# A two-layer streaming encoder step: an opening that requests less, the indexer's and the selection's work laid out anew, and head loads of 128 partitions

## The chip, the cores and the metric

The program runs on one core of one Trainium2 chip. The metric is the device time of one execution in microseconds (us), the median of several. A profile of a single execution stands beside it. In what follows PE is TensorE, DVE is VectorE, ACT is ScalarE, POOL is GpSimd and SP is SyncE, which here issues nearly all DMAs. The profile counts 16 DMA engines for the core.

## The reference

One inference step of a trunk of two layers on two groups of rows: one prompt of 1024 rows, and 8 samples of 16 new rows (128 rows in all), each with 512 cached rows. The width is 1024.

```python
for layer in range(2):
    mod = silu(c) @ ada_w[layer] + ada_b[layer]
    shift, scale, gate = split(mod, 3)
    h = rms_norm(x, norm_g[layer]) * (1 + scale) + shift
    y = mixer(h)                 # layer 0: mixer_ab, layer 1: mixer_c
    x = x + gate * y
return rms_norm(x, final_norm_g)

def mixer_ab(h):                 # layer 0
    qa, ka, va, fa, ga, qb, kb, vb, iq, ik, iw, gb = split(h @ w_in)
    # A: 8 heads of 64, softmax(q k / 8 + cum_f[q] - cum_f[k]), causal
    # B: 8 heads of 64; indexer: score[q, k] = sum_h iw[q, h] * relu(iq[q, h] . ik[k]);
    #    the 256 best keys of a prompt row (132 of a sample row) are attended to
    return concat(oa * silu(ga), ob * silu(gb)) @ w_out
```

Layer 1 is a latent attention of 16 heads, which the change leaves alone. Keys, values, gates of forgetting and indexer keys are outputs too.

## The kernel before

All rows stand in 9 tiles of 128 (8 of the prompt, 1 of the samples). Products that need full precision are made of three passes, from a tensor split into a high and a low part (`product`, L274 to L276).
- **`opening`** loads the rows x, the first ada_w matrix (8 pieces of 1 MB, L114) and the weights of the first projection (`entry.fetch_weights`, L397). PE multiplies the pieces (L212), DVE places the modulation (L231, L234). Behind the weights SP also issues the rope tables (L116, L117), three more ada_w tiles through `Modulation.load` (L256 to L259, each after `w_used`), two short tables and a bias (L121 to L123).
- **`projection("ix")`** with `front=entry` makes the indexer's queries and keys. ACT first rounds weight pieces (`split_high`, L618), DVE subtracts (`split_low`, L694), four of eight pieces before the first row tile's `front.act` / `front.dve` and four behind it. PE turns row tiles (L317) and starts its products when all pieces are split. DVE applies rope (L843 to L846). Two MB of the modulation are multiplied beside it (L267).
- **`index_scores`** has 48 steps (6 row tiles, 8 heads): PE a product (L1020), ACT a relu (L1064), DVE a weighted sum (L1133). Between them stands the samples' work for batches b = 0 to 7, at steps given by dictionaries: PE turns cached keys at step 6+5b (L981), ACT and DVE split them at 7+5b (L1078, L1143), PE scores at 9+5b, ACT's relu at 10+5b, PE's sum at 11+5b (L995). The new keys' scores (24 products of 16 columns), their relu and sum stand behind the last step. ACT waits for the samples' queries and keys at step 5 (L1068).
- **`projection("ab")`** has 8 groups of 9 steps, in this order: copy, copy, copy, silu, rope, rope, copy, silu. A step is 24 products of PE; ACT moves a copy (L642) or makes the three passes of a silu (L648, L650, L652), DVE multiplies it (L718) or applies rope. Groups with a turned output (1, 2, 5 and 6) add four transposes, an ACT and a DVE operation (L674, L753) to each step. Beside this DVE runs the top-k selection, 7 row tiles wide: `idle` takes 4 of its 259 passes per step. 231 of them are counts of about 0.9 us (L1191) and the last 28, four per tile, turn the threshold into a mask (L1225 to L1238).
- **`branches_ab`** is the attention of layer 0: 16 heads g (8 of A, 8 of B), each with 8 row tiles of the prompt and one sample batch. SP loads, per head, queries and keys (`at_q`, `at_k`, L1338 and L1340; each half of the partitions holds the same 64 key rows, the halves of the queries are the high and low part), the decay row for A (L1344), values (L1347), cached keys (L1355), the additive row (`at_addt`, L1362), cached values (L1365) and the new values (L1366). Three buffers of queries and keys, two of the rest.
- Then come `mixed_out`, the projection, attention and output of layer 1.

The additive row is read through a pattern of the source whose outermost count is 8:

```python
rows = dram(c.s["negcum_s"], h * H * KEYS, [[KEYS, H], [0, TS], [1, KEYS]])   # H = 8, TS = 16
sp.dma_start(addt[:, g % 2], rows)
```

Of the kernel before, what the change touches and what calls it, by code (L numbers as in the profile page):

```python
# [7 lines left out]

# [13 lines left out]
P = 128  # L22
# [3 lines left out]
NB = 8  # L26
# [57 lines left out]
def opening(nc, c, x_tile, entry):  # L84

    S = lambda name: semaphore(nc, name)
    rows_in, g_in, bias_in, w_in, rope_in = S("mod_rows_in"), S("mod_g_in"), S("mod_bias_in"), [S(f"ada_w_in{i}") for i in range(AW)], S("rope_in")
# [6 lines left out]
    with ExitStack() as stack:  # L94
# [8 lines left out]
        def _(sp):  # L103
# [12 lines left out]
            sp.dma_start(c.ropeC[:], c.i["rope_cos"].rearrange("(i p) d -> p i d", p=P)).then_inc(rope_in, 16)  # L116
            sp.dma_start(c.ropeS[:], c.i["rope_sin"].rearrange("(i p) d -> p i d", p=P)).then_inc(rope_in, 16)  # L117
# [3 lines left out]
            sp.dma_start(c.ropeCs[:], c.i["rope_cos_short"].rearrange("(i p) d -> p i d", p=P)).then_inc(entry.tables_in, 16)  # L121
            sp.dma_start(c.ropeSs[:], c.i["rope_sin_short"].rearrange("(i p) d -> p i d", p=P)).then_inc(entry.tables_in, 16)
            sp.dma_start(c.fbias[:], dram(c.i["ab_f_bias"], 0, [[0, P], [1, H]])).then_inc(entry.tables_in, 16)  # L123
            sp.wait_ge(rope_in, 32)
# [27 lines left out]
        def _(act):  # L152
# [3 lines left out]
            for n in range(3):  # L156
# [7 lines left out]
                nc.scalar.activation(rstd[:, cols], ss[:, cols], ACT.Sqrt, scale=1.0 / D, bias=c.eps[:]).then_inc(std, 1)  # L164

# [56 lines left out]
AW = 3  # L222

# [146 lines left out]
class Entry(Rows):  # L370

    READY, SPLIT = 0, False

    def __init__(self, nc, c, w_dram, col, stack):
# [3 lines left out]
        self.w_hi, self.w_lo, self.tables_in = semaphore(nc, "ix_w_hi"), semaphore(nc, "ix_w_lo"), semaphore(nc, "tables_in")  # L378
# [5 lines left out]
    def place(self, side):  # L384
        sb = lambda n, shape, dt=F32: self.stack.enter_context(self.nc.sbuf_tensor(n, shape, dt))
        self.side = side
        with self.nc.sbuf_tensor("mod_x_first", [P, 2, D], F32) as self.x_first:
            pass
        self.T = sb("ix_T", [P, 2, 2, 4, P], F32R)
        self.x_rows = sb("mod_x_rows", [P, NT - 3, D])  # L390

# [7 lines left out]
    def enter(self, stack):  # L399
        super().enter(stack)  # L400
        self.wh = stack.enter_context(self.nc.sbuf_tensor("ix_wh0", [P, KT, 512], F32R))
# [17 lines left out]
class Front(Rows):  # L419

    READY, SPLIT = 1, True
# [50 lines left out]
def projection(nc, c, name, groups, idle=None, pair=BF16, ring=4, side=None, front=None, weights=None, sums=None):  # L472
# [36 lines left out]
    with ExitStack() as stack:  # L509
# [105 lines left out]
        def _(act):  # L615
# [3 lines left out]
            ahead = 0 if front and front.SPLIT else groups[0].kt  # L619
            for k in range(ahead // 2 if front else ahead):  # L620
                split_high(0, k)
            for i in range(2 if front else 0):
                front.act(act, i)
                if i == 0:
                    for k in range(ahead // 2, ahead):
# [57 lines left out]
        def _(dve):  # L683
# [11 lines left out]
            ahead = 0 if front and front.SPLIT else groups[0].kt  # L695
            for k in range(ahead // 2 if front else ahead):
# [3 lines left out]
            for i in range(2 if front else 0):  # L700
                front.dve(dve, i)
                if i == 0:
                    for k in range(ahead // 2, ahead):
                        split_low(0, k)
            for s in range(len(steps) + LAG):
                if front and s < len(steps):
                    front.dve(dve, s + 2)
                if s < len(steps) and groups[steps[s][0]].kind != "copy":
# [10 lines left out]
                    if kind == "rope":  # L719
                        rope(nc, chain, o, ps, turn[:, 0:n], c.ropeC[:, i, :], c.ropeS[:, i, :], n // DH, DH // 2).then_inc(nat_done, 1)  # L720
# [160 lines left out]
def index_scores(nc, c, sums, weights):  # L881
# [14 lines left out]
    turn_at, score_at, sum_at = {6 + 5 * b: b for b in range(NB)}, {9 + 5 * b: b for b in range(NB)}, {11 + 5 * b: b for b in range(NB)}  # L896
    high_at, relu_at = {7 + 5 * b: b for b in range(NB)}, {10 + 5 * b: b for b in range(NB)}
    NEW_ROW = 12
    assert max(sum_at) < N + 1
    with ExitStack() as stack:  # L900
# [57 lines left out]
        def _(pe):  # L958
# [45 lines left out]
            for s in range(N + 1):  # L1004
                if s < N:
                    i, h = steps[s]
                    m = s // H
                    if s == 0:
                        pe.wait_ge(k_done, 1)
# [1541 lines left out]
```

## Time and profile before

| | |
|---|---|
| median of 3 runs | 1937.97 us (1937.79 to 1943.93) |
| the profiled execution | 1940.82 us |
| its span, first to last instruction | 1939.1 us |
| mean granted TensorE clock | 0.940 |
| PE busy | 1689.8 us, 87% of the span |
| DVE busy | 1297.3 us, 67% |
| ACT busy | 941.7 us, 49% |
| DMA queue of SP and ACT, share of 16 engines | 38.3% |

The stages in the profile, by the times at which their first instructions start: opening 0 to 55.4 us, projection ix to 183, index_scores to 279.1, projection ab to 724.4, attention of layer 0 to 1049.4, the rest to 1939.1. A row of the list of DMA issues ends with the KB of one and, where the profile has it, the median time to landing. In a row of the timeline an engine name with a q (SPq) is its queue of issues; the text in brackets is the idle time before the instruction and what ended it. Granted clock 1.00 is 2.4 GHz, 0.50 is 1.2 GHz. A row of a window's sums holds its bounds, its length, the busy time (and count) of PE, PE's weight loads, DVE, ACT and POOL, and then the granted clock, the DMA share (mean busy share of the 16 DMA engines) and the GB/s that they moved.

### The profile page before, as it was taken

Reading aid. Unit: us, or ns where it says so; the run is one execution under the profiler, and the core shown is the slowest. Engines: PE = TensorE matmul, PEld = TensorE weight load, DVE = VectorE, ACT = ScalarE, POOL = GpSimd, SP = SyncE. Lnnn points to the kernel's source line nnn. Section 1 sums busy time; section 2 is a strip of 40 time slices with the busy share of each in tenths; the row PEclk is TensorE's granted clock in tenths of the full one; section 3 lists DMA queues with packets and bytes.
Section 4 is the critical chain, followed back from the end, with each engine's and each line's share of the span. In section 5 each row is a group of like instructions: output and inputs, shape, how many; then the busy total and the mean of one; then the engine's idle time right before and its main releaser. Section 6 shows DMA issues by size and latency. Waiting matters only on the chain. (4 is left out here: it accounts for less than half of the span.)

```text
span 1939.1 us, 34317 instructions
## 1 busy us (share of the span) xinstructions
PE 1689.8 (87%) x12754; PEld 1314.9 (68%) x12754; DVE 1297.3 (67%) x2825; ACT 941.7 (49%) x1897; POOL 209.0 (11%) x310
## 2 busy tenths in 40 slices
PE   3794789999998966899998998889996999999798
PEld 0572458888877854677776787677774776676687
DVE  0553577878999934678888655553365777777764
ACT  2422552227211364577876225447644676777421
POOL 2001100010000002101010000000004222221000
PEclk7797899999999987899998998989997999999899
DMA  9366511432233119968774643232235111111432
GB/s 347 116 211 191 121 39 51 130 105 88 74 98 107 62 55 223 227 195 217 198 197 147 230 172 119 70 110 96 73 79 117 28 28 45 27 28 51 152 130 98
DMA packets 229550, 235.17 MB, mean 121 GB/s; under 512 B 139350, under 2 KB 164214, under 8 KB 227339
## 3 DMA queue, kind: packets, MB, share of 16 engines
q1 hardware_dynamic: 222506, 213.07, 38.3%
q0 software_dynamic: 6880, 19.92, 2.8%
q8 instruction: 103, 1.69, 0.4%
q14 instruction: 61, 0.49, 0.1%
HBM read 173.98 MB, written 58.95 MB: 120 GB/s over the span
## 5 line engine op out<-in xcount | busy, mean ns | idle before, releaser
L274 PE MATMUL PS<-ab_wh,hT 128*128 128x512 f32 x576 | 231.4, 402 | 5.7 <-DVE ab_wl L694 5.7
L275 PE MATMUL PS<-ab_wl,hT 128*128 128x512 f32 x576 | 227.3, 395 | 0.0
L276 PE MATMUL PS<-ab_wh,hT 128*128 128x512 f32 x576 | 226.6, 393 | 0.0
L1191 DVE TENSOR_SCALAR_CACHE_REDUCE topk_junk<-scores,topk_small 128x528 bf16<-128x528 f32 (+6 forms) x224 | 194.6, 916 | 1.3
L2368 DVE CUSTOM_DVE_ANT_0 la_S<-PS,la_mask 128x128 f32<-128x128 f32 (+3 forms) x144 | 107.5, 747 | 41.5 <-PE PS L276 28.5
L274 PEld LDWEIGHTS PS<-ab_wh,hT 128*128 128x128 f32 x576 | 109.4, 190 | 29.2 <-ACT ab_wh L618 3.9
L276 PEld LDWEIGHTS PS<-ab_wh,hT 128*128 128x128 f32 x576 | 109.2, 190 | 25.0
L1541 ACT ACTIVATE at_P<-at_S,at_nm 128x128 f32<-128x128 f32 (+2 forms) x144 | 110.5, 767 | 29.5 <-DVE at_nm L1586 29.3
L275 PEld LDWEIGHTS PS<-ab_wl,hT 128*128 128x128 f32 x576 | 109.3, 190 | 22.1
L274 PE MATMUL PS<-out_wh,out_mT 128*128 128x512 f32 x288 | 116.1, 403 | 4.7 <-DVE out_mT L1844 4.7
L2290 ACT ACTIVATE la_P<-la_S,la_nm 128x128 f32<-128x128 f32 (+3 forms) x144 | 110.4, 767 | 9.3 <-DVE la_nm L2368 9.2
L275 PE MATMUL PS<-out_wl,out_mT 128*128 128x512 f32 x288 | 114.2, 396 | 0.0
L276 PE MATMUL PS<-out_wh,out_mT 128*128 128x512 f32 x288 | 114.0, 396 | 0.0
L2386 DVE TENSOR_TENSOR la_PT<-PS,la_PT 128x512 bf16<-128x512 f32 (+1 forms) x192 | 100.8, 553 | 19.0 <-ACT la_PT L2304 17.7
L1436 PE MATMUL PS<-at_k,at_q 128*128 128x512 bf16 (+3 forms) x384 | 89.2, 343 | 27.3 <-DMA at_k<-scratch_kaT 20.2
L2304 ACT ACTIVATE la_PT<-PS 128x512 bf16<-128x512 f32 (+1 forms) x192 | 87.0, 488 | 51.6 <-PE PS L2191 48.7
L1596 DVE TENSOR_TENSOR at_PT<-PS,at_PT 128x512 bf16<-128x512 f32 (+1 forms) x192 | 100.9, 553 | 15.9 <-ACT at_PT L1555 14.5
L1555 ACT ACTIVATE at_PT<-PS 128x512 bf16<-128x512 f32 (+1 forms) x192 | 86.9, 487 | 49.3 <-PE PS L1462 49.2
L1462 PE MATMUL PS<-ident,at_P 128*128 128x128 f32 (+1 forms) x656 | 103.5, 281 | 3.2 <-DVE at_PT L1596 2.4
L2191 PE MATMUL PS<-ident,la_P 128*128 128x128 f32 (+1 forms) x656 | 97.0, 275 | 6.6 <-DVE la_PT L2386 6.6
L642 ACT ACTIVATE ab_nat<-PS 128x512 f32<-128x512 f32 x36 | 21.5, 598 | 154.6 <-PE PS L276 145.0
L274 PE MATMUL PS<-c_wh,hT 128*128 128x512 f32 x216 | 87.3, 404 | 0.0
(424 smaller groups left out, 4437.3 us busy)
## 6 DMA issues: line engine op xcount, KB each, us to landing
mod_ada_w<-in_ada_w SPq DMA_DIRECT2D x16, 1024.0 KB, 6.6
ab_wl_raw<-in_ab_w_in SPq DMA_DIRECT2D x64, 256.0 KB, 4.8
out_g<-scratch_gates_nat SPq DMA_DIRECT2D x18, 512.0 KB, 5.3
mod_ada_w<-in_ada_w SPq DMA_DIRECT2D x16, 512.0 KB, 5.0
at_kc<-in_cache_a_k SPq DMA_DIRECT2D x8, 1024.0 KB, 8.9
at_vc<-in_cache_a_v SPq DMA_DIRECT2D x8, 1024.0 KB, 7.5
at_kc<-in_cache_b_k SPq DMA_DIRECT2D x8, 1024.0 KB, 7.7
at_vc<-in_cache_b_v SPq DMA_DIRECT2D x8, 1024.0 KB, 5.3
```

The costliest lines, as they stand in the source:

```text
L274: nc.tensor.matmul(out, x[0], w[0], start=start, stop=False)
L275: nc.tensor.matmul(out, x[0], w[1], start=False, stop=False)
L276: return nc.tensor.matmul(out, x[1], w[0], start=False, stop=stop)
L1191: go(V.tensor_scalar(mark, x, limit, 0.0, op, ALU.add, accum_out=cnt[:, m:m + 1]), 0 if m == M - 1 else 1)
L1436: last = nc.tensor.matmul(PS[:, to + a // 512, 0:w], q[:, g % 3, i * P:(i + 1) * P], k[:, g % 3, d, a:a + w], start=d == 0, stop=d == 1 an ...
L1462: last = nc.tensor.transpose(PS[0:w, bank(u), b * P:(b + 1) * P], Psb[:, s % 2, at:at + w], c.ident[:])
L1541: nc.scalar.activation(Psb[:, s % 2, 0:widths(s)], Ssb[:, s % 2, 0:widths(s)], ACT.Exp, bias=nm[:, s:s + 1], scale=-1.0, accum_out=total). ...
L1596: nc.vector.tensor_tensor(lo, PS[:, bank(u), 0:n * P], hi, ALU.subtract).then_inc(unit_free[u % 3], 1)
L2191: last = nc.tensor.transpose(PS[0:w, bank(m), b * P:(b + 1) * P], Psb[:, s % 2, at:at + w], c.ident[:])
L2290: nc.scalar.activation(Psb[:, s % 2, 0:widths(s)], Ssb[:, s % 2, 0:widths(s)], ACT.Exp, bias=nm[:, s:s + 1], scale=-1.0, accum_out=total). ...
L2368: nc.vector.tensor_tensor_reduce(Ssb[:, s % 2, 0:widths(s)], flat(s), tile, -1.0, 3e38, ALU.add, ALU.min, nm[:, s:s + 1]).then_inc(maxed, 1)
L2386: nc.vector.tensor_tensor(lo, PS[:, bank(m), 0:n * P], hi, ALU.subtract).then_inc(unit_free[m % 3], 1)
```

## The change

It has four parts. (1) The opening's SP list ends with the first projection's weights; tables and modulation tiles are issued by SP in the next block (`fetch_tables`). ACT rounds the first 5 weight pieces at the end of the opening; the next block rounds 3 behind the first row tile, and DVE subtracts 3 before it and 5 behind. (2) In `index_scores` the samples' work moves to steps 10+4b and so on, ACT's wait from step 5 to 9, and the new keys' work into steps 42, 44 and 46. (3) `selection` spreads the 259 passes by the kind of step: weights 4.4 for a copy, 4.0 for a silu, 2.0 for a rope. (4) Queries and keys of a head are loaded by 3 DMAs of 128 partitions.

```diff
@@ opening, SP
             entry.fetch_weights(sp)
-            sp.dma_start(c.ropeC[:], ...).then_inc(rope_in, 16)
-            sp.dma_start(c.ropeS[:], ...).then_inc(rope_in, 16)
-            for n in range(AW):
-                sp.wait_ge(w_used, KT - AW + n + 1)
-                entry.side.load(sp, n)
-            sp.dma_start(c.ropeCs[:], ...).then_inc(entry.tables_in, 16)
-            sp.dma_start(c.ropeSs[:], ...).then_inc(entry.tables_in, 16)
-            sp.dma_start(c.fbias[:], ...).then_inc(entry.tables_in, 16)
-            sp.wait_ge(rope_in, 32)
@@ opening, ACT
+            for k in range(EARLY):            # EARLY = 5
+                entry.split_high(act, k)
@@ class Entry
+    def fetch_tables(self, sp):
+        sp.dma_start(c.ropeC[:], by_tile("rope_cos")).then_inc(self.rope_in, 16)
+        sp.dma_start(c.ropeS[:], by_tile("rope_sin")).then_inc(self.rope_in, 16)
+        for n in range(AW):
+            self.side.load(sp, n)
+        sp.dma_start(c.ropeCs[:], by_tile("rope_cos_short")).then_inc(self.tables_in, 16)
+        sp.dma_start(c.ropeSs[:], by_tile("rope_sin_short")).then_inc(self.tables_in, 16)
+        sp.dma_start(c.fbias[:], dram(c.i["ab_f_bias"], 0, [[0, P], [1, H]])).then_inc(self.tables_in, 16)
@@ projection, SP, and DVE at rope
+            if side:
+                front.fetch_tables(sp)
+                        if side and s == 0:
+                            dve.wait_ge(front.rope_in, 32)
@@ index_scores
-    turn_at, score_at, sum_at = {6 + 5 * b: b ...}, {9 + 5 * b: b ...}, {11 + 5 * b: b ...}
-    high_at, relu_at = {7 + 5 * b: b ...}, {10 + 5 * b: b ...}
+    at = lambda first: {first + 4 * b: b for b in range(NB)}
+    turn_at, high_at, score_at, relu_at, sum_at = at(10), at(11), at(15), at(16), at(19)
+    NEW_ROW, NEW_KEYS, NEW_RELU, NEW_SUM = 12, 42, 44, 46
@@ selection
+ROOM = {"copy": 4.4, "silu": 4.0, "rope": 2.0}
+    room = [ROOM[g.kind] for g in groups for _ in range(NT)]
+    until = lambda s: math.ceil(topk.passes() * sum(room[:s + 1]) / sum(room[:-1]))
-        for _ in range(-(-topk.passes() // (n - 2)) if s < n - 1 else topk.passes()):
+        for _ in range(until(s) - (until(s - 1) if s else 0) if s < n - 1 else topk.passes()):
@@ branches_ab, SP
-                for half in range(2):
-                    sp.dma_start(q[DH * half:DH * (half + 1), g % 3, :], qT[x][half, h * DH:(h + 1) * DH, 0:SEQ]).then_inc(head_in[g % 3], 16)
-                    for d in range(2):
-                        sp.dma_start(k[DH * half:DH * (half + 1), g % 3, d, :], kT_dram[x][d, h * DH:(h + 1) * DH, 0:SEQ]).then_inc(head_in[g % 3], 16)
+                sp.dma_start(q[:, g % 3, :], dram(qT[x], h * DH * TOK, [[HD * TOK, 2], [TOK, DH], [1, SEQ]])).then_inc(head_in[g % 3], 16)
+                for d in range(2):
+                    sp.dma_start(k[:, g % 3, d, :], dram(kT_dram[x], (d * HD + h * DH) * TOK, [[0, 2], [TOK, DH], [1, SEQ]])).then_inc(head_in[g % 3], 16)
```

In SP's list the first head's loads stood so before, where `out_wl_raw` is the buffer that holds the decay row and `out_g` the one that stages the samples' queries and keys:

```order
L1338 DMA at_q<-scratch_qaT 64x1024
L1340 DMA at_k<-scratch_kaT 64x1024 x2
L1338 DMA at_q<-scratch_qaT 64x1024
L1340 DMA at_k<-scratch_kaT 64x1024 x2
L1344 DMA out_wl_raw<-scratch_negcum_p 128x1024
L1347 DMA at_v<-out_p_a_v 128x8x64
L1355 DMA at_kc<-in_cache_a_k 128x4x512
L1362 DMA at_addt<-scratch_negcum_s 128x1x528
```

And now:

```order
L1358 DMA at_q<-scratch_qaT 128x1x1024
L1360 DMA at_k<-scratch_kaT 128x1x1024 x2
L1364 DMA out_wl_raw<-scratch_negcum_p 128x1024
L1367 DMA at_v<-out_p_a_v 128x8x64
L1375 DMA at_kc<-in_cache_a_k 128x4x512
L1382 DMA at_addt<-scratch_negcum_s 128x1x528
```

Six DMAs of 64 partitions became three of 128, of the same form as the one of `at_addt`; the sources' patterns now begin with a count of 2.

On DVE, near the end of projection ab, the last selection passes stood so before (two tiles' masks, then the silu group's multiplications, L718):

```order
L718 TENSOR_TENSOR ab_nat<-PS,ab_tmp 128x512
L1232 TENSOR_SCALAR topk_w<-scores,topk_small 128x1024
L1233 SCALAR_TENSOR_TENSOR scores<-topk_ones,topk_w 128x1024
L1235 SCALAR_TENSOR_TENSOR topk_w<-scores,topk_small,topk_w 128x1024
L1236 TENSOR_TENSOR topk_w<-topk_w,topk_junk 128x1024
L1238 TENSOR_SCALAR scores<-topk_w 128x1024
L718 TENSOR_TENSOR ab_nat<-PS,ab_tmp 128x512 x7
```

And now:

```order
L1241 TENSOR_SCALAR scores<-scores,topk_small 128x1024
L1207 TENSOR_SCALAR topk_junk,topk_small<-scores,topk_small 128x1024
L1246 TENSOR_TENSOR topk_small<-topk_small 128x1
L725 TENSOR_TENSOR ab_nat<-PS,ab_tmp 128x512
L1248 TENSOR_SCALAR topk_w<-scores,topk_small 128x1024
L1249 SCALAR_TENSOR_TENSOR scores<-topk_ones,topk_w 128x1024
L1251 SCALAR_TENSOR_TENSOR topk_w<-scores,topk_small,topk_w 128x1024
L1252 TENSOR_TENSOR topk_w<-topk_w,topk_junk 128x1024
L1254 TENSOR_SCALAR scores<-topk_w 128x1024
L725 TENSOR_TENSOR ab_nat<-PS,ab_tmp 128x512
```

All 28 mask passes moved into the last group: one tile's four between each two multiplications, the last ones just ahead of the last multiplication, where seven multiplications stood behind them before.

## Rows read from the trace of the kernel before

**Rows 1.** Sums by window: the opening, projection ab, layer 0's attention

```profile
0.00:55.40 55.40, 16.54 (x77) 3.31 (x78) 4.17 (x16) 13.27 (x25) 13.37 (x30) 0.76 0.96 352
...
279.10:724.40 445.30, 419.41 (x1872) 341.22 (x1872) 368.15 (x823) 154.97 (x227) 29.24 (x54) 0.98 0.27 87
724.40:1049.40 325.00, 286.28 (x4000) 220.49 (x4000) 237.85 (x576) 224.85 (x544) 41.46 (x63) 0.93 0.76 194
```

**Rows 2.** Timeline at the opening's end: start us, duration us, what

```profile
32.90 5.01 SPq L397 DMA_DIRECT2D ix_wl_raw<-in_ab_w_in  x8
44.13 0.29 DVE L234 SCALAR_TENSOR_TENSOR modT<-PS,gT 128x36 f32<-128x36 f32 x2
51.99 2.94 SPq L123 DMA_DIRECT2D fbias<-in_ab_f_bias  x1
...
55.39 2.19 ACT L618 ACTIVATE ix_wh<-ix_wl_raw 128x512 fp32r<-128x512 f32 x4 [34.75 <-PEq L94]
55.42 1.94 PE L317 MATMUL PS<-ident,mod_x_first 128*128 128x128 f32 x8 [11.54 <-PEq L94]
```

**Rows 3.** Landing of the first weights' DMAs (L397), from issue

```profile
DMA to landing us min/median/max: 7.7/8.0/8.2
```

**Rows 4.** index_scores: a relu, ACT's wait, PE's score products, the stage's end

```profile
197.84 0.49 ACT L1064 ACTIVATE is_rel<-PS 128x384 f32<-128x384 f32 x1 [0.46 <-PE PS L1020]
...
204.47 2.00 ACT L1068 ACTIVATE is_qs<-is_qs_raw 64x1024 fp32r<-64x1024 f32 x2 [5.49 <-DMA is_kn_raw<-scratch_ikT]
...
L274 PE MATMUL PS<-is_kcT,is_qs 64*128 64x512 f32 x8 | 4.0, 501 | 6.9 <-DVE is_kcT L1143 6.9
...
272.16 1.20 PE L1020 MATMUL PS<-is_k,is_q 128*128 128x512 f32 x4
277.00 0.71 DVE L1151 COPY scores<-PS 128x528 f32<-128x528 f32 x1 [1.08 <-PE PS L995]
```

**Rows 5.** Projection ab: ACT where a step of PE ends, the rope stretch, DVE's counts

```profile
299.23 0.60 ACT L642 ACTIVATE ab_nat<-PS 128x512 f32<-128x512 f32 x1 [3.91 <-PE PS L276]
305.22 0.60 ACT L642 ACTIVATE ab_nat<-PS 128x512 f32<-128x512 f32 x1 [4.39 <-PE PS L276]
...
488.72 0.60 ACT L648 ACTIVATE ab_tmp<-PS 128x512 f32<-128x512 f32 x1 [0.43 <-PE PS L276]
...
633.48 0.60 ACT L642 ACTIVATE ab_nat<-PS 128x512 f32<-128x512 f32 x1 [3.34 <-PE PS L276]
639.03 0.60 ACT L642 ACTIVATE ab_nat<-PS 128x512 f32<-128x512 f32 x1 [4.43 <-PE PS L276]
...
528.00:624.00 96.00, 85.88 (x382) 68.01 (x381) 93.55 (x212) 14.17 (x25) 5.94 (x11) 0.96 0.29 85
...
L1191 DVE TENSOR_SCALAR_CACHE_REDUCE topk_junk<-scores,topk_small 128x528 bf16<-128x528 f32 (+6 forms) x224 | 194.6, 916 | 1.3
```

**Rows 6.** DVE: first and last mask pass, the stage's last multiplication

```profile
643.91 0.49 DVE L1225 TENSOR_SCALAR scores<-scores,topk_small 128x528 f32<-128x528 f32 x1
...
692.00 0.69 DVE L1238 TENSOR_SCALAR scores<-topk_w 128x1024 f32<-128x1024 f32 x1
...
715.62 0.69 DVE L718 TENSOR_TENSOR ab_nat<-PS,ab_tmp 128x512 f32<-128x512 f32 x1 [3.67 <-ACT ab_tmp L652]
```

**Rows 7.** Windows with one kind of transfer: at_vc, then at_addt, then at_q/at_k

```profile
895.00:896.00 1.00, 1.00 (x10) 0.73 (x9) 0.72 (x3) 1.00 (x4) 0.00 (x0) 1.00 1.05 399
957.10:957.70 0.60, 0.60 (x11) 0.59 (x8) 0.60 (x2) 0.53 (x3) 0.00 (x0) 1.00 0.53 208
916.00:917.00 1.00, 1.00 (x13) 0.74 (x9) 0.98 (x3) 1.00 (x3) 0.00 (x0) 1.00 1.07 229
```

**Rows 8.** at_addt's DMA issues of 850 to 1000 us, from the list of issues

```profile
at_addt<-scratch_mask_s SPq DMA_DIRECT2D x7, 264.0 KB
```

**Rows 9.** SP's last two loads of the first head's keys; a window's sums

```profile
726.85 1.24 SPq L1340 DMA_DIRECT2D at_k<-scratch_kaT  x2
...
744.00:764.00 20.00, 17.55 (x241) 13.62 (x239) 13.46 (x31) 13.58 (x32) 2.98 (x9) 0.89 1.08 231
```

More of the change, by code:

```diff
@@ L9 @@
+import math
 import numpy as np
@@ L222 @@
 AW = 3
+EARLY = 5
 def place_modulation(nc, c, l, a, turned, j):
@@ L618, in split_high @@
                 nc.scalar.activation(wh[slot(g)][:, k, 0:groups[g].n], raw[slot(g)][:, k, 0:groups[g].n], ACT.Copy).then_inc(w_hi, 1)
-            ahead = 0 if front and front.SPLIT else groups[0].kt
-            for k in range(ahead // 2 if front else ahead):
+            for k in range(0 if front else groups[0].kt):
                 split_high(0, k)
@@ L624, in _ @@
                 if i == 0:
-                    for k in range(ahead // 2, ahead):
+                    for k in range(front.HIGH, groups[0].kt):
                         split_high(0, k)
@@ L694, in split_low @@
                 nc.vector.tensor_tensor(wl[slot(g)][:, k, 0:n], raw[slot(g)][:, k, 0:n], wh[slot(g)][:, k, 0:n], ALU.subtract).then_inc(w_lo, 1)
-            ahead = 0 if front and front.SPLIT else groups[0].kt
-            for k in range(ahead // 2 if front else ahead):
+            first_low = 0 if front and front.SPLIT else front.LOW if front else groups[0].kt
+            for k in range(first_low):
                 split_low(0, k)
@@ L701, in _ @@
                 front.dve(dve, i)
-                if i == 0:
-                    for k in range(ahead // 2, ahead):
+                if i == 0 and not front.SPLIT:
+                    for k in range(first_low, groups[0].kt):
                         split_low(0, k)
@@ new lines, in sum_new @@
+            def sum_new():
+                pe.wait_ge(new_read, 1)
+                pe.wait_ge(tr_read, 3)
+                for b in range(NB):
+                    last = weighted(b, 7, TS, rs_new[:, b, :])
+                last.then_inc(new_sum, 1)
+            for s in range(N):
+                i, h = steps[s]
+                m = s // H
+                if s == 0:
+                    pe.wait_ge(k_done, 1)
+                if i * P == 512 and h == 0:
+                    pe.wait_ge(k_done, 2)
+                if s >= 2:
+                    pe.wait_ge(relu_done, s - 1)
+                if h == 0:
+                    pe.wait_ge(q_done, m + 1)
+                n = (i + 1) * P
+                for a in range(0, n, 512):
+                    w = min(512, n - a)
+                    for d in range(2):
+                        last = nc.tensor.matmul(PS[:, 2 * (s % 2) + a // 512, 0:w], q[:, m % 3, h, :], k[:, d, a:a + w],
+                                                start=d == 0, stop=d == 1)
+                last.then_inc(mm_done, 1)
@@ L1031, in _ @@
                     sum_sample(sum_at[s])
[L1032 to L1041 removed]
+                if s == NEW_KEYS:
+                    score_new()
+                if s == NEW_SUM:
+                    sum_new()
         @block.scalar
@@ L2500, in build @@
                 c.topk.small = inner.enter_context(nc.sbuf_tensor("topk_small", [P, 9, len(SELECT_TILES) + 1], F32))
-                projection(nc, c, "ab", groups, selection(nc, c), weights=weights)
+                projection(nc, c, "ab", groups, selection(nc, c, groups), weights=weights)
             retire_semaphores(nc)
```

84 lines of the change are left out of this document (28 added, 56 removed).

## Prediction

> **What bounds the kernel now.** I read the window sums by stage first. In the opening PE works 16.5 of 55.4 us and the DMA engines are 96% busy [rows 1]. In projection ab it works 419.4 of 445.3 us, in the attention of layer 0 286.3 of 325.0 at a DMA share of 0.76. So the attention runs close to PE, with DMA not far behind. The timeline then says what each idle time is. The opening's last computation ends at 44.42, yet its block ends only after SP's last issue at 54.93, and PE starts at 55.42 [rows 2]. In index_scores ACT waits 5.5 us for the samples' keys, and PE's score products 6.9 us for DVE's split of cached keys [rows 4]. In projection ab PE loses its time in the rope groups, where DVE is 93.6 of 96 us busy and PE 85.9 [rows 5].
>
> **Part 1, the opening.** SP's list there now ends with the weights at 37.91. DVE's end at 44.42 then closes the block, if ACT's five rounded pieces are not later. The fifth piece is issued at about 32.90 + 4 x 0.63 = 35.4 and lands 8.0 later, at 43.4 [rows 2, 3]. One piece takes 2.19 / 4 = 0.55, so ACT ends at about 44.0, just in time. From SP's end to PE's start the block change took 55.42 - 54.93 = 0.49. The next block starts at 44.9, not 55.4: 10.5 us earlier. In it DVE must still make the same 8 subtractions before the products can start, but starts 0.6 sooner, since its first three pieces are already rounded; against that it waits once more for ACT. I take 0.2. Sum: **-10.7**. The 4 MB that SP now issues later take some 12 us at the opening's 352 GB/s [rows 1]. What hides them is that their first user, rope, stands behind the first step's 24 products, and these behind two row tiles and DVE's eight subtractions. If that cover is gone, up to 12 us are lost again; I hold it safe. If the weights land 2 us later than I say, the gain is 2 us less. Bounds: -7 and -11.5.
>
> **Part 2, index_scores.** ACT's wait moves four steps on. A relu takes 0.49, with up to 0.46 of idle before it, and the tiles widen from step 8 on: steps 6 to 9 last 0.8 to 1.0 each, so 3.6 of the 5.5 are filled. The score products now stand 5 steps behind the turned keys, not 3, which removes most of the 6.9; some of that comes back as work that PE must now put in fewer steps, so I take 5. Behind the last product (ends 273.36) stood 3.6 us up to DVE's copy at 277.0; now DVE's last sum of 1.3 and relu of 1.0 stand there, 1.1 less, but 2.9 us of new-key products go between the steps, where half of it finds PE waiting. I take -0.4 for this. Sum: **-9** (bounds -4 and -13) [rows 4].
>
> **Part 3, the selection.** From 488.72 (a silu group's last step) to 633.48 lie 22 steps, 144.8 us [rows 5]. Without a wait 18 of them would take 5.99 and 4 would take 5.55: 130.0. So the rope groups cost PE 14.8 us. The waits lie in the stretch of 528 to 624, some 13 steps of 5.99 + 14.8 / 13 = 7.1, DVE's pace. A pass is a count of 0.92 with its share of small operations, 0.94; 2.03 passes fewer leave DVE 5.2 a step, below 5.99: the 14.8 go. Outside that stretch DVE is busy (368.2 - 93.6) / (445.3 - 96) = 79% [rows 1, 5], and 0.34 passes more, 0.3 us, find room. But the stage does not end with PE. The 28 mask passes took DVE from 643.91 to 692.69 [rows 6], 48.8 us, of which 3.6 were splits and multiplications: 45.2. They now stand wholly in the last group, with the last three counts, of the widest tiles, and four small operations (4.1) and nine multiplications of 0.6 (5.5): 54.8 us in one unbroken run on DVE. It starts when the group's first silu leaves ACT. A silu takes ACT 4.4 us (the last multiplication's 0.69 and the 3.67 before it [rows 6]); with 0.2 for the hand-over that is 4.6 behind PE's step 63. This step ended five steps behind 639.03, at 666.7, and now at 666.7 - 14.8 = 651.9. So the last multiplication ends at 651.9 + 4.6 + 54.8 = 711.3, against 716.31 before: **-5.0**. What PE gains, DVE takes back; behind the group DVE is late next, and PE stands idle for some 16 us at the end. Bounds -9 and 0.
>
> **Part 4, the heads.** This part decides. Bytes stay (768 KB a head); three issues of 0.6 us fall away, which on SP are in nobody's way except at the first head, whose first product waits for the sixth issue, which ends at 728.09 [rows 9]: 1.9 us, counted with the start below. What changes is the pattern: the source now begins with a count of 2. No row of before shows such a load, but one is of the same form, at_addt, whose source begins with a count of 8. While it alone moves, the DMA engines show a share of 0.53 and 208 GB/s; at_vc, whose source begins with 128, shows 1.05 and 399 [rows 7]. Half the engines at the full rate of each: 8 of 16. Its row in the list of issues also ends without a landing time [rows 8], as if not all engines reported. By that a count of 2 keeps the load on **two engines**, 50 GB/s. 786,432 bytes then take 15.8 us a head. Upper bound: at_q and at_k now move at 229 GB/s with a share of 1.07 [rows 7], 14.3 per engine; at that rate of each engine, 27.5 us. Lower bound: at_addt's 26 per engine, 15.1. I take 15.8, since 64 partitions are what sets at_q apart from the other two, and that goes.
>
> The two engines must do their part of all else too. In the stage the engines are busy 0.76 x 325 = 247 us, 15.4 per head [rows 1]; at_q and at_k are 786,432 / 229,000 x 1.07 = 3.7 of it; the rest is 11.7 (lower bound, all other 2.9 MB at 399: 7.3). Two engines are thus busy 15.8 + 11.7 = 27.5 us per head, where a head now takes 325 / 16 = 20.3. The buffers let SP run a head ahead, so these engines never rest, and PE waits for each head. 16 x 27.5 = 440, plus 2 for the first issues and 7 for what of the last head follows its loads: 449 against 325, **+124**. Bounds: 16 x 22.4 + 9 = 367, +42; and 16 x 39.2 + 9 = 636, +311.
>
> The Trainium skill, "DMA: Bandwidth & Descriptors", says the same in "Why a DMA increments its semaphore by 16 and not by 1": the engines used are the largest number up to 16 that divides the slowest dimension of both patterns, and a leading zero-stride count confines a load. At its roughly 27 GiB/s an engine the head would take an estimated 13.6 us instead of 15.8. Its "Rules for kernel authors" also advise one 128-partition transfer for two halves, which speaks for the change; the trace's at_addt row decides for me.
>
> **Sum.** 1940.8 - 10.7 - 9 - 5.0 + 124 = 2040.1. The median of the runs lies 2.9 below the profiled execution: **2037**.
>
> **Rivals.**
> (a) The count does not matter, and 128 partitions go over all engines. For it: at_q's 229 GB/s at a full share [rows 7] is 64 partitions' rate, which 128 could lift, and among the first heads the DMA share is 1.08 [rows 9]. Against it: at_addt's row. Then 24.7 + 1.9 are gained, and some 3 in the crowded first heads: 1937.9 - 29.6 = 1908. It decides if the loads keep over half of the engines. The skill's rule of one 128-partition transfer would give this. Chance 0.12.
> (b) Two engines, and PE's clock falls as well. From 744 to 764, among the first heads, PEclk was 0.89 with PE busy 17.6 of 20 us [rows 9], which speaks against it. PE needs 286 / 16 = 17.9 us a head; with most of it at 1.2 GHz it would need about 33, more than 27.5: 16 x 33 + 9 = 537, 2125. Chance 0.12.
> (c) Each of the two engines keeps today's slower rate of at_q: +311, 2224. Chance 0.06.
> (d) The loss just eats the gain of 25: two engines whose work is mostly hidden. Chance 0.02.
> The forecast itself: 0.68.
>
> **Numbers.** About 0.3%, 6 us, is what a measurement can tell from no change. Faster 0.12 (a), same 0.02 (d), slower 0.86. The forecast's own range is 1995 (15.1 + 10 a head, +86) to 2100 (20 + 11.7 a head, +190); with (b) it reaches to 2135. Range 1992 to 2135.
>
> **What would show it.** Right: in the attention the DMA share falls to about 0.4 to 0.5 while its stage grows to some 450 us, at_q and at_k take over 15 us to land or have no landing time, and PE waits for at_k at every head. The projection ix starts at 44.9. In projection ab PE idles nowhere in the rope groups, and DVE's masks run until 5 us behind everything else. Wrong: if at_k lands in 3 us as before, part 4 falls, and the kernel is faster.

## The result and the profile after

The changed kernel takes **2045.75 us** (median of 4 runs, 2043.75 to 2050.29) against 1939.26 for the kernel before (4 runs): a ratio of 1.0548, 95% interval 1.0521 to 1.0575. That is 106.5 us more; the prediction said 99 more, 2037.

The sums by window, stage by stage. Columns: from:to, length, busy time of PE, PE's weight loads, DVE, ACT and POOL with instruction counts, granted clock, DMA share, GB/s. The stages are the opening, projection ix, index_scores, projection ab, layer 0's attention.

```profile
0.00:43.20 43.20, 15.27 (x77) 3.25 (x77) 4.17 (x16) 16.29 (x29) 13.36 (x30) 0.85 0.92 359
43.20:170.30 127.10, 102.86 (x542) 69.36 (x542) 67.55 (x169) 33.54 (x73) 5.08 (x10) 0.88 0.62 192
170.30:262.80 92.50, 73.20 (x293) 45.71 (x293) 58.47 (x84) 51.40 (x78) 7.46 (x17) 0.80 0.42 90
262.80:703.80 441.00, 414.07 (x1872) 339.57 (x1872) 368.92 (x823) 155.16 (x227) 29.23 (x54) 0.97 0.28 88
703.80:1157.00 453.20, 306.81 (x3968) 248.24 (x4000) 239.91 (x576) 227.18 (x544) 41.34 (x63) 0.80 0.48 139
```

In [rows 1] the opening took 55.4 us and the attention 325.0. The attention is now 128.2 us longer, with the DMA share down from 0.76 to 0.48: nearly everything is decided there. The timeline of SP's queue for one head of B shows how (start us, us, what):

```profile
1000.62 0.50 SPq L1358 DMA_DIRECT2D at_q<-scratch_qbT  x1
1001.17 10.66 SPq L1360 DMA_DIRECT2D at_k<-scratch_kbT  x2
1011.88 5.12 SPq L1367 DMA_DIRECT2D at_v<-out_p_b_v  x1
1017.04 5.28 SPq L1375 DMA_DIRECT2D at_kc<-in_cache_b_k  x1
1022.36 1.29 SPq L1382 DMA_DIRECT2D at_addt<-scratch_mask_s  x1
...
1026.58 0.50 SPq L1358 DMA_DIRECT2D at_q<-scratch_qbT  x1
```

One head's loads are issued 26.0 us after the last head's. In the kernel before, the keys' issues took 0.6 each, those of values and cached keys 0.6 and 0.4; here two of the keys' take 10.66, and those behind them up to 5.3: SP itself is now held at its queue. The windows of the same head show what the DMA engines do meanwhile, and where PE stands still:

```profile
1007.00:1017.00 10.00, 9.79 (x125) 7.65 (x126) 8.87 (x23) 7.63 (x18) 0.00 (x0) 1.00 0.13 49
1021.00:1026.90 5.90, 0.00 (x0) 0.00 (x0) 0.14 (x1) 0.04 (x1) 0.00 (x0) 0.69 0.71 206
```

For 10 us the share is 0.13 at 49 GB/s. That is two sixteenths of the engines' time, so two engines at 25 GB/s each. Then PE is idle for 5.9 us. PE's waits in the attention name the load it stands for (us in total, times, longest):

```profile
PE PS L1456 <- DMA at_k<-scratch_kaT: 67.0, 7, 43.7
PE PS L1456 <- DMA at_k<-scratch_kbT: 52.1, 8, 8.9
```

These are 15 waits for 16 heads. The longest one, 43.7, is the first head's. It begins at PE's last product of projection ab, so 24.2 us of it lie in the stage before.

And the list of issues has no landing time for at_k or at_q, as at_addt had none in [rows 8]:

```profile
at_k<-scratch_kaT SPq DMA_DIRECT2D x16, 256.0 KB
...
at_q<-scratch_qaT SPq DMA_DIRECT2D x8, 256.0 KB
at_v<-out_p_a_v SPq DMA_DIRECT2D x8, 256.0 KB, 12.2
```

The opening's end, against [rows 2]. DVE's last computation ends at 42.7 and PE starts the next block at 43.26:

```profile
42.41 0.29 DVE L229 SCALAR_TENSOR_TENSOR modT<-PS,gT 128x36 f32<-128x36 f32 x2
...
43.26 1.94 PE L312 MATMUL PS<-ident,mod_x_first 128*128 128x128 f32 x8 [1.10 <-PEq L95]
```

In index_scores ACT's wait of [rows 4] for the samples' loads is gone. Another wait, for the third tile of the prompt's queries, now ends last there. (The kernel before had it too, 7.36 us long, see part 2 below.)

```profile
193.88 0.69 DVE L1120 CAST is_q<-is_q_raw 128x1024 fp32r<-128x1024 f32 x1 [7.20 <-DMA is_q_raw<-scratch_iqT]
...
195.19 1.32 ACT L1079 ACTIVATE is_rel<-PS 128x512 f32<-128x512 f32 x2 [7.40 <-DVE scores L1149]
```

In projection ab PE has no idle time over the stretch of the rope groups and more. At the stage's end stand 24.2 us without any work of PE, up to the first issue of the attention:

```profile
440.00:624.00 184.00, 184.00 (x841) 151.02 (x840) 162.85 (x360) 61.65 (x91) 12.95 (x24) 1.00 0.30 95
...
679.60:703.80 24.20, 0.00 (x0) 0.00 (x0) 15.62 (x17) 4.42 (x5) 1.62 (x3) 0.55 0.08 33
```

DVE's last operations, on the timeline:

```profile
694.27 0.69 DVE L1254 TENSOR_SCALAR scores<-topk_w 128x1024 f32<-128x1024 f32 x1
695.00 0.69 DVE L725 TENSOR_TENSOR ab_nat<-PS,ab_tmp 128x512 f32<-128x512 f32 x1
```

### The profile page after: what moved, and what is told of

It reads as the page before. It is cut to its first block and busy times, and to the rows that moved or that the text cites. A ratio compares the mean times of both kernels' runs of the same rounds, so it can differ in the third digit from the quotient of the medians.

```text
span 2042.6 us, 34198 instructions
## 1 busy us (share of the span) xinstructions
PE 1701.1 (83%) x12683; PEld 1342.9 (66%) x12754; DVE 1300.0 (64%) x2825; ACT 945.3 (46%) x1897; POOL 208.9 (10%) x310
## 5 line engine op out<-in xcount | busy, mean ns | idle before, releaser
L1456 PE MATMUL PS<-at_k,at_q 128*128 128x512 bf16 (+3 forms) x352 | 83.6, 346 | 123.1 <-DMA at_k<-scratch_kaT 67.0
L1482 PE MATMUL PS<-ident,at_P 128*128 128x128 f32 (+1 forms) x656 | 119.5, 316 | 38.9 <-DVE at_PT L1616 38.9
L1456 PEld LDWEIGHTS PS<-at_k,at_q 128*128 128x128 bf16 x384 | 34.9, 103 | 141.4 <-issue 80.7
L1482 PEld LDWEIGHTS PS<-ident,at_P 128*128 128x128 f32 (+1 forms) x656 | 86.7, 162 | 53.2 <-DVE at_PT L1616 42.2
```

What stands on the lines that cost most here:

```text
L1456: last = nc.tensor.matmul(PS[:, to + a // 512, 0:w], q[:, g % 3, i * P:(i + 1) * P], k[:, g % 3, d, a:a + w], start=d == 0, stop=d == 1 an ...
L1482: last = nc.tensor.transpose(PS[0:w, bank(u), b * P:(b + 1) * P], Psb[:, s % 2, at:at + w], c.ident[:])
```

## The experiments

Each is told by its ratio to the kernel before, measured beside it on the same chip, with a 95% interval. Differences in us are worked out from these ratios where nothing else is said.

### heads_alone: part 4 on the kernel before

The kernel before with these lines, and the semaphore's wait at 48 per use where 96 stood:

```diff
-                for half in range(2):
-                    sp.dma_start(q[DH * half:DH * (half + 1), g % 3, :], qT[x][half, h * DH:(h + 1) * DH, 0:SEQ])...
-                    for d in range(2):
-                        sp.dma_start(k[DH * half:DH * (half + 1), g % 3, d, :], kT_dram[x][d, h * DH:(h + 1) * DH, 0:SEQ])...
+                sp.dma_start(q[:, g % 3, :], dram(qT[x], h * DH * TOK, [[HD * TOK, 2], [TOK, DH], [1, SEQ]]))...
+                for d in range(2):
+                    sp.dma_start(k[:, g % 3, d, :], dram(kT_dram[x], (d * HD + h * DH) * TOK, [[0, 2], [TOK, DH], [1, SEQ]]))...
```

> The kernel before with only part 4: queries and keys of layer 0's heads in 3 transfers whose source begins with a count of 2. Theory A (a leading count of 2 keeps each load on two of the 16 DMA engines, and these set the pace of a head): the attention stage takes 16 x 27 + 9, some 445 to 455 us in place of 325, and the kernel comes to 1939 + 128 = 2067, at least 2055. Theory B (the changed kernel is slow only because its other parts now let the attention start against the late end of the selection, or because of PE's lower clock): less than 60 of the 106 us lost, below 2000.

Measured: 2067.58 us, ratio 1.0676 (1.0655 to 1.0697), +131 us. The attention in its profile:

```profile
726.50:1178.90 452.40, 301.99 (x3968) 244.17 (x4000) 240.11 (x577) 227.50 (x545) 41.44 (x63) 0.80 0.47 139
```

The stage is as long as in the changed kernel. The heads' loads alone carry the whole loss and more; the other parts do not cause it, they win back some of it elsewhere.

### all_but_heads: the changed kernel with the six transfers of before

The diff above, taken back.

> The changed kernel with the six transfers of 64 partitions of before. Theory A: the attention is back at 325 us and what remains are parts 1 to 3, measured in the changed kernel's profile as 12.2 + 2.4 + 5.4 = 20 us: 1919, between 1914 and 1922; my forecast of these parts was 24.7 less, 1914. Theory B: part of the loss stays, over 1940.

Measured: 1920.18, ratio 0.9915 (0.9898 to 0.9931), -16.5 us. Parts 1 to 3 together are a gain, within what was expected here and smaller than the 24.7 that I had forecast. In its profile the attention takes 318.4 us. With the same loads it takes 325.0 in the kernel before and 321.1 to 325.3 in the profiles of opening_alone, index_alone and selection_alone: a difference of a few us in this stage means little.

### heads_64x2: the same three transfers, leading counts exchanged

Against the changed kernel:

```diff
-                sp.dma_start(q[:, g % 3, :], dram(qT[x], h * DH * TOK, [[HD * TOK, 2], [TOK, DH], [1, SEQ]]))...
+                sp.dma_start(q[:, g % 3, :], dram(qT[x], h * DH * TOK, [[TOK, DH], [HD * TOK, 2], [1, SEQ]]))...
                 for d in range(2):
-                    sp.dma_start(k[:, g % 3, d, :], dram(kT_dram[x], (d * HD + h * DH) * TOK, [[0, 2], [TOK, DH], [1, SEQ]]))...
+                    sp.dma_start(k[:, g % 3, d, :], dram(kT_dram[x], (d * HD + h * DH) * TOK, [[TOK, DH], [0, 2], [1, SEQ]]))...
```

The products sum over the partitions, so an order that queries and keys share changes nothing in them.

> The changed kernel, still 3 transfers of 128 partitions and the same bytes, but the two leading counts of the source change places: first the 64 rows, then the 2 halves (for keys the repeat), so that partition 2r and 2r + 1 hold row r; queries and keys use the same order. Theory A: the leading count is 64, all 16 engines work, the attention takes 325 us or a few less, 1914 to 1921. Theory C (it is the form that costs: one transfer on 128 partitions, or reading each row of the keys twice by a stride of zero, wherever that stands): the loss stays, 2040 to 2050.

Measured: 1906.78, ratio 0.984 (0.9818 to 0.9861), -30 us against the kernel before and -13 against all_but_heads, by the medians. Neither 128 partitions nor the repeat by a stride of zero brings any loss. It is faster than any of my theories had it. Windows of its profile, a stretch of head loads alone and the first 61 us of the attention, and of all_but_heads those first 61 us:

```profile
905.00:907.00 2.00, 2.00 (x25) 1.74 (x24) 1.67 (x5) 1.82 (x6) 0.00 (x0) 1.00 1.04 404
703.70:765.00 61.30, 46.22 (x592) 35.95 (x599) 37.31 (x92) 36.02 (x89) 19.40 (x34) 0.81 0.97 286
```

```profile
705.40:767.00 61.60, 39.48 (x485) 30.14 (x493) 30.33 (x74) 29.77 (x73) 13.96 (x28) 0.79 0.99 230
```

With all engines busy, a share of about 1.0, they move 404 GB/s into 128 partitions where they moved 229 into 64 [rows 7]. A head's 786,432 bytes take all engines 1.9 us, not 3.4. The first heads, where the share is 1.0, get shorter: the second to fifth head start 17.2 to 21.5 us apart, where all_but_heads needed 18.6 to 26.1. The last four distances are all 17.0 or 17.1, in all_but_heads 17.0 to 18.0.

### halves_count2 and halves_count4: the count alone

Six transfers of 64 partitions each, no row read twice; only the order in which the rows are named:

```diff
-                    sp.dma_start(q[DH * half:DH * (half + 1), g % 3, :], qT[x][half, h * DH:(h + 1) * DH, 0:SEQ])...
+                    sp.dma_start(q[DH * half:DH * (half + 1), g % 3, :], dram(qT[x], (half * HD + h * DH) * TOK, [[TOK, 2], [2 * TOK, DH // 2], [1, SEQ]]))...
```

(the keys likewise; in halves_count4 the 2 is a 4).

> The changed kernel with six transfers of 64 partitions and no row read twice, but each source begins with a count of 2: the 64 rows are taken as 2 x 32, even rows first, then odd ones, for queries and keys alike. Theory A: again two engines, 2040 to 2052. Theory C (128 partitions or the stride of zero costs): as all_but_heads, 1914 to 1922.

> As halves_count2, but each source of 64 rows begins with a count of 4 (4 x 16 rows). Theory A, with the number of engines that this count gives: a load that runs alone shows a DMA share of 0.25 and 100 GB/s, where the changed kernel showed 0.13 and 49; a head costs these four engines 7.9 us of loads and the 10 to 12 us of the rest that the changed kernel's heads left over (26 to 27.7 measured, less 15.8), some 19.8 for layer a's heads and 18.3 for b's, so most of the loss is gone: attention 325 to 335 us, the kernel 1920 to 1935. Rival: any count below 16 confines the loads to the same two engines, 2045 to 2055.

Measured: halves_count2 2054.17, ratio 1.0606 (1.0584 to 1.0628), two us above the expected range and some 10 above the changed kernel. Those 10 do not lie in the attention, which takes the same 453 us:

```profile
712.30:1166.10 453.80, 303.56 (x3968) 245.53 (x4000) 239.86 (x577) 227.36 (x545) 41.43 (x63) 0.81 0.47 139
```

In its profile the opening, index_scores and the stages behind the attention, where it is the same code, took 4.5, 2.9 and 3.6 us more. halves_count4 took 1942.7, ratio 1.0025 (1.001 to 1.0039): 21 us above all_but_heads. Windows with head loads alone, first of halves_count2:

```profile
1017.00:1024.00 7.00, 6.94 (x74) 5.69 (x75) 6.34 (x15) 5.71 (x15) 0.00 (x0) 1.00 0.13 50
```

and of halves_count4:

```profile
934.30:937.90 3.60, 3.60 (x40) 2.64 (x33) 2.60 (x8) 2.57 (x8) 0.00 (x0) 1.00 0.27 86
```

PE's waits in halves_count4's attention, for the keys (the 36.8 is the first head's again, and begins in the stage before):

```profile
PE PS L1457 <- DMA at_k<-scratch_kaT: 38.0, 2, 36.8
PE PS L1457 <- DMA at_k<-scratch_kbT: 10.0, 5, 3.5
```

Share 0.13 with a count of 2, 0.27 with 4: the share follows the count, and the rival that any count below 16 gives two engines fell. halves_count4 came out above its expected 1920 to 1935, and its attention, 343.0 us, above 325 to 335; why was not tried. Of the heads of B the last four distances are 18.9 to 20.7 us, where I had worked out 18.3 and where all_but_heads needs 17.0 to 18.0.

### selection_alone, opening_alone, index_alone: parts 3, 1 and 2 on the kernel before

Each is the kernel before with that part of the change and no other.

> The kernel before with the pacing of the selection alone. My step: -5.0 against the kernel before (the changed kernel's trace gave -5.4 for the stage). Rival: DVE's masks at the end take back all, 0; or all of the rope groups' 14.8 us is kept, -15.

> The kernel before with the changed opening alone (the tables and later weights requested in the projection, five pieces rounded early). Forecast -10.7; the changed kernel's profile gives -12.2 for the start of the projection's block and -12.5 for its first product: 1926, ratio 0.9938 (0.993 to 0.995). If the 4 MB that it puts off slow the projection: -2, ratio 0.999.

> The kernel before with the changed index_scores alone. My forecast of the part was -9; the changed kernel's profile gives -2.4 for the stage. If that holds alone: 1935.5 against 1938, ratio 0.9988. If the forecast part was right and the other parts took it back: -9, ratio 0.9954.

Measured: selection_alone 1932.56, ratio 0.9967 (0.9953 to 0.9982), -6.4 us. opening_alone 1927.59, ratio 0.9947 (0.993 to 0.9963), -10.3 us. index_alone 1937.52, ratio 0.9997 (0.9979 to 1.0015), -0.6 us, which can't be told from nothing, nor from the -2.4. The sizes of the first two held. The forecast -9 of the third is excluded.

The stage of index_scores (first issue to the next stage's first product) is itself not the same in every execution. With the old layout it takes 97.6 to 99.1 us in four profiles. With the new one, the run of new-key products undivided, it takes 94.9 to 95.2 in six and 98.0 to 99.1 in three (halves_count2, even_masks, index_alone). Those three have one more stretch of 6.8 us at 1.2 GHz in the middle of the stage, here in index_alone:

```profile
221.40:228.20 6.80, 6.80 (x17) 3.82 (x16) 3.31 (x5) 1.42 (x3) 0.00 (x0) 0.50 0.01 4
```

### queries_first: which landing is late in index_scores

```diff
             load_q(1)
+            load_q(2)
             sp.dma_start(kc[:], c.i["cache_b_idx_k"]...)
...
-            load_q(2)
             sp.wait_ge(logf_done, 1)
```

> heads_64x2 with one pair of issues moved: in index_scores SP issues the third queries tile before the cached keys and the samples' queries and keys, not behind them. The changed kernel's trace shows ACT's wait of 5.5 us gone from there, but DVE's cast of these queries waiting 7.2 us for their landing at 193.86, and ACT and PE behind it. Theory D (part 2 fell short because this landing is late next, 1.3 us behind the one removed): the stage gets 5 us shorter (7.2 less some 1.5 in which ACT now waits for the samples' queries); against heads_64x2 -5, between -3 and -7. Theory E (all these landings are held by the DMA engines' share of 1.15 and the order decides nothing, or the fall of PE's clock behind 248 takes it): under 2 us.

Measured: 1903.65, ratio 0.9822 (0.9805 to 0.9839), which overlaps that of heads_64x2, and the stage is as long in both profiles (95.0 and 94.9 us up to the first product of the next). Theory D fell, and what theory E said of the order held. The timeline shows why:

```profile
189.21 0.69 DVE L1120 CAST is_q<-is_q_raw 128x1024 fp32r<-128x1024 f32 x1
...
196.48 2.00 ACT L1083 ACTIVATE is_qs<-is_qs_raw 64x1024 fp32r<-64x1024 f32 x2 [4.64 <-DMA is_kn_raw<-scratch_ikT]
196.50 1.06 PE L990 MATMUL PS<-ident,is_kc 128*64 128x128 f32 x4 [4.59 <-DMA is_kn_raw<-scratch_ikT]
```

The queries no longer wait, but ACT and PE do, until 196.48. The stage's first issue stands at 172.85 here and at 170.29 in the changed kernel: 23.6 us in both cases (193.88 - 170.29 and 196.48 - 172.85). Whichever load is put last lands at 23.6. For most of that time the DMA engines are busy throughout, and SP is held 7.0 us at one issue, where the second one of the same form takes 0.6. Both in the changed kernel, an issue and a window's sums:

```profile
177.61 6.98 SPq L944 DMA_DIRECT2D is_qs_raw<-scratch_iqT  x1
...
175.30:190.30 15.00, 8.22 (x24) 4.86 (x21) 4.28 (x8) 7.30 (x12) 4.63 (x8) 0.61 1.19 195
```

The order of the requests decides who waits, and, as far as these two runs show, their sum how long.

### even_masks and both: the tail of projection ab

```diff
     room = [ROOM[g.kind] for g in groups for _ in range(NT)]
+    room[-NT:] = [2.7] * NT
```

on heads_64x2; "both" has this and queries_first.

> heads_64x2 with the weight of the last silu group in the pacing at 2.7 where 4.0 stood, so that some 22 passes lie before the group's last step, not 31, and the seven earlier groups take 9 more. Theory F (in projection ab DVE's masks alone set the end, PE being done with its last product at 679.6 of 703.8): the last group then needs 22 x 1.6 + 8 x 0.6 = 40 us of DVE, below PE's 43.5, the last multiplication follows PE's last product by some 6 us, and the stage ends 10 us sooner: against heads_64x2 -10, between -6 and -12. Theory G (9 more passes make the copy groups' steps bound by DVE, 4.46 passes x 0.94 + 0.69 + 0.6 = 5.5 us against steps of 5.4 to 6.0): PE idles in groups 1 to 7 and the gain is under 4.

> heads_64x2 with both edits, queries_first and even_masks. The two stages are apart, so the gains add: -15 against heads_64x2, between -9 and -19; the kernel near 1891.

Measured: even_masks 1898.98, ratio 0.9797 (0.9778 to 0.9817), -8 us against heads_64x2; both 1892.98, ratio 0.9783 (0.9763 to 0.9803), -11, or -14 by the medians. In even_masks' profile projection ab takes 429.7 us from its first product to the attention's first issue, in heads_64x2's 438.5: 8.8 less. PE's busy time there is the same 414, and its last product comes no later after the first; DVE's last multiplication now follows it by 7.7 us, not 16.1. The stage's window, and that multiplication on the timeline:

```profile
272.00:702.00 430.00, 413.85 (x1872) 339.38 (x1872) 368.36 (x823) 154.60 (x227) 29.59 (x54) 0.98 0.29 90
```

```profile
693.81 0.69 DVE L725 TENSOR_TENSOR ab_nat<-PS,ab_tmp 128x512 f32<-128x512 f32 x1
```

Theory F held, within its range. The intervals of "both" and even_masks overlap, so that the further 3 us (6 by the medians) may be nothing. They can't be the queries' order, since index_scores is not shorter in "both" (95.1 us) than in heads_64x2. even_masks' own profile has 3 us more in index_scores, from the stretch at 1.2 GHz told above, and 3 in the opening, where it is the same code.

### new_in_four: the run of short products

On "both": the products for the samples' new keys at steps 42 to 45, a quarter at each.

```diff
-    NEW_ROW, NEW_KEYS, NEW_RELU, NEW_SUM = 12, 42, 44, 46
+    NEW_ROW, NEW_KEYS, NEW_RELU, NEW_SUM = 12, 42, 46, 47
...
-                if s == NEW_KEYS:
-                    score_new()
+                if NEW_KEYS <= s < NEW_KEYS + 4:
+                    score_new(s - NEW_KEYS)
```

> The kernel both, with the 48 products of 16 columns for the samples' new keys in four parts of 12, at four successive steps, where they stood in one run at one step; the relu and the sum of them two and one step later. Every kernel with the changed index_scores shows the granted clock at 1.00 up to the end of this run and at 0.63 over the 9.2 us behind it. Theory H (the run of short products is what the fall of the clock follows): the clock stays at 1.00 there and the stage of index_scores ends some 3 us sooner, about 1890 against 1893. Theory I (the clock falls there for another reason, such as the steady work before): it falls at about the same place, and nothing is gained.

The traces show 24 such products (8 batches of three), six a part, where the expectation said 48 and 12. Measured: 1894.04, ratio 0.976 (0.9738 to 0.9783), whose interval meets that of "both". The profiles are plainer. The kernel both, ahead of, during and behind the run:

```profile
242.30:247.30 5.00, 4.81 (x17) 2.44 (x16) 3.66 (x5) 3.38 (x5) 0.00 (x0) 1.00 0.00 0
247.30:250.10 2.80, 2.80 (x25) 2.75 (x24) 2.39 (x2) 1.18 (x2) 0.00 (x0) 1.00 0.00 0
250.10:259.30 9.20, 9.01 (x22) 4.76 (x21) 2.30 (x3) 2.92 (x5) 0.00 (x0) 0.63 0.00 0
```

and new_in_four, ahead of and over the four parts:

```profile
240.20:245.20 5.00, 4.81 (x17) 2.43 (x16) 3.65 (x5) 3.38 (x5) 0.00 (x0) 1.00 0.02 3
245.20:253.60 8.40, 8.40 (x43) 5.67 (x42) 5.14 (x4) 4.44 (x6) 0.00 (x0) 1.00 0.00 0
```

In "both" the clock granted to PE is at its full 2.4 GHz until the run is over and then for most of 9.2 us at 1.2 GHz. With the run in four pieces it stays at 2.4 GHz, and the stage takes 91.5 us to the next one's first product, not 95.1. No other profile has this stage under 94.9. Theory H held in the profile, a single one, and by an edit that also moves the relu and the sum a step or two; the intervals of the two kernels can't tell the 3.6 us.

## Why the prediction was right, and where it was not

**Part 4, two engines.** Right, in mechanism and in size. I gave 27.5 us a head and +124; measured are heads 27.9 us apart in A (from the second, 752.9, to the ninth, 948.5) and 26.1 in B, a stage of 453.2 us, +128. It is 452 to 454 us in all three kernels whose loads begin with a count of 2. The step from at_addt's row [rows 7, 8] to a count of 2 is what carried it: the share went from 0.53 at a count of 8 over 0.27 at 4 to 0.13 at 2. The two rates that I had chosen between, 15 to 27.5 us for a head's own loads, came out at the low end: 49 GB/s over two engines is 16.0 us. For the other transfers I had 11.7. What the measured 27.9 and 26.1 leave for them is 11.9 and 10.1. The DMA share of one head of B checks this without that difference:

```profile
948.50:974.40 25.90, 19.70 (x245) 15.72 (x248) 16.75 (x40) 14.92 (x36) 1.94 (x3) 0.81 0.47 136
```

0.47 of 16 engines over 25.9 us is 195 us of engine time. Two engines spend 16.0 each on the head's queries and keys; the rest, spread over 16, is an estimated 10.2 each. So the two are busy for about 26.2 of 25.9 us: they never rest, as forecast. The 4 us that were missing lie at the ends. PE waits 19.4 us for the first head's load, where I had put 2. Against that the heads start 27.2 us apart on average, not 27.5, and the last head takes 26 us from its start, not 34.5. The Trainium skill, "DMA: Bandwidth & Descriptors", in its section "Why a DMA increments its semaphore by 16 and not by 1", has the number of engines as the largest one up to 16 that divides the slowest dimension of both patterns; the counts 2, 4 and 64 in these runs agree with it (shares 0.13, 0.27 and 1.04). That the count and not the form of the transfer is the cause is shown by heads_64x2 and halves_count2, which change either without the other.

**The rivals.** (a), that the count does not matter, fell, but its mechanism is real: transfers to 128 partitions move at 404 GB/s. I had given it some 3 us in the crowded first heads; heads_64x2 shows -13 in the medians and -16 in the attention of its profile (302.8 for 318.4). The same page of the Trainium skill advises one 128-partition transfer over two halves ("Rules for kernel authors"); the runs agree as soon as the leading count is 64 (0.984 against 0.9915 for the halves). (b): the clock did fall, 0.80 in the stage where 0.93 was granted before, and PE was busy 306.8 us for 286.3. But it falls where PE idles behind the missing keys, and 306.8 stays far below 453. With the two engines' work filling the whole distance between heads, I read it as a consequence and not the bound. (c) and (d) fell. In the part on numbers two bounds are some 4 us too low: by the terms given, 1995 is 1999 and 2100 is 2103; the "20" in the second has no row behind it.

**Part 1, -10.7.** Right: -10.3 alone. The block's start came at 43.2, not 44.9, since DVE's last computation itself ended 1.7 us sooner in this execution; in the ten profiles with the new opening PE's first product there starts at 42.1 to 47.7. The 4 MB put off stayed hidden: the projection has 127.1 us where it had 127.6.

**Part 2, -9.** Wrong, outside its bounds in the profile: nothing measurable alone, -2.4 in the changed kernel's profile. Two steps failed. First, "so 3.6 of the 5.5 are filled" took ACT's wait for the only one there. The waits of the kernel before had another:

```profile
DVE is_q L1104 <- DMA is_q_raw<-scratch_iqT: 13.9, 3, 7.4
...
ACT is_qs L1068 <- DMA is_kn_raw<-scratch_ikT: 5.5, 1, 5.5
```

DVE's wait of 7.4 us ended with the same batch of loads; the third queries' cast started 23.7 us into the stage before and 23.6 after. I read the wait that the change takes away, and not what else ended at that time. Second, the new keys' products between the steps were booked as 2.9 us of work that half finds PE waiting; what they cost besides is the clock behind them, 3.6 us by new_in_four's profile. The last queries' cast, 60.2 us into the stage before and 55.8 after, was 4.4 us ahead; at the stage's end 2.4 are left. So, by the place in the stage, the term of 3.6 came to 0.1, the term of 5 to 4.3, and the term of -0.4 to +2.0. And the clock's extra stretch in some executions (3 us) is larger than what is left.

**Part 3, -5.0.** Right: -5.4 in the profile, -6.4 alone. The last step of the last copy group left PE at 630.6 instead of 661.2, 30.6 us sooner, of which the stage's start gives 15.2 and the rope groups 15.4 (forecast 14.8); DVE's masks then ended the stage, with PE's last product 16.1 us before the last multiplication (forecast some 16).

**The sum.** In the profiles the misses of part 2 (7 us too good) and of part 4 (4 too small), less the 1.9 us that parts 1 and 3 gave more, come to 9 us, the size of the 9 us between 2037 and 2045.75. That they fit so well is partly luck. In the profiles the stages behind layer 0's attention, which the change leaves alone, took 4.1 us less (885.6 for 889.7), and projection ix 0.5 less. In return the median lies 1.4 us above the profiled execution, where I had set it 2.9 below. The parts measured alone add up to +114 (131 - 10.3 - 6.4 - 0.6, each by its ratio); the kernel shows +106. With intervals of 3 to 5 us to either side on each of the five numbers, that is not told apart from a plain sum.

## What to carry to other kernels

Before merging transfers, read the leading count of both patterns: where it is as small as the 8, 4 and 2 here, look in the trace for a load of the same form, and at its DMA share while it runs alone. Another order of the same dimensions, shared by both operands of a product, can give the long transfer and all engines: here the kernel with 2 x 64 rows is 106 us slower than the one before, and the same kernel with 64 x 2 is 30 us faster, 13 of them by this form of load. Where a wait for a load is taken away, list all waits that end at about the same time; if the DMA share is near 1 up to that point, moving requests only changes who waits. And where PE gets faster, pace the other engine's leftover work against the new step, not the old one: that gave a further 8 us, and the best version run here, "both" with the short products in four parts, is 2.4% faster than the kernel before (0.976).

## What the runs showed of the hardware

- The same 786,432 bytes at a DMA share of 1.04 to 1.07 move at 404 GB/s into 128 partitions and at 229 into 64. Yet two engines alone move 25 GB/s each into 64 partitions (halves_count2), and four 21.5, against 14.3 for each of sixteen. So the slow rate into 64 partitions is not a fixed limit of each engine: an engine's rate falls with the number that write at once. What it lies in was not tried.
- Loads that are confined to a few engines hold the issuing queue too: SP's issue of two keys' loads took 10.66 us, where 1.24 was enough for two before, and the loads behind it, for all engines, started that much later.
- A run of 24 products of 16 columns, 2.8 to 3.3 us of a fully busy PE, went with a fall of PE's clock to 1.2 GHz for 6.8 to 10.2 us in all 13 profiles that have it. In eleven the fall came 0.1 to 2.4 us behind the run's end, in heads_alone and index_alone 1.0 and 1.1 us ahead of it. (In four of the 13, those with the old layout, the run ends the stage and PE goes idle soon after, so they say less.) With the same products in groups of six (new_in_four, one profile) it did not come. The clock also falls elsewhere in this stage without such a run, as in the 6.8 us shown above, so the run is not the only cause. Why the clock follows it was not tried.
